# Four places instead of five for the first token tile's expert rows, and the freed memory for six weight tiles loaded early

## The chip, the cores and the metric

The kernel runs on one core of one Trainium2 chip. The metric is the device time of one execution in microseconds (us). The kernel before took 2138.37 us, the median of three runs (2136.37 to 2140.15).

## What is computed

One layer of a decoder block for 256 tokens of width 2048, all in fp32, with weights read from HBM. A token mixer (sparse attention and latent attention, merged by gates) is followed by a channel mixer that looks up experts:

```python
h = rms_norm(x, attn_pre_g[l]) * (1 + sc_a) + sh_a
y = token_mixer(h, positions, w_in[l], ...)          # ends: merged @ w_out
x = x + g_a * rms_norm(y, attn_post_g[l])
h = rms_norm(x, ffn_pre_g[l]) * (1 + sc_f) + sh_f
y = peer_ffn(h, peer_w_q[l], peer_sub_keys[l], peer_u[l], peer_v[l])
x = x + g_f * rms_norm(y, ffn_post_g[l])
```

In `peer_ffn` each token has 8 heads, and each head picks 16 of 16384 experts (two top-16 searches over 128 sub-keys, then a top-16 of their 256 sums). An expert has a row of `u` and a row of `v`, 2048 numbers each:

```python
act = jax.nn.gelu(jnp.einsum('cd,ced->ce', hs, u[es]))
return jnp.einsum('ce,ced->cd', gs * act, v[es])
```

So each of 256 tokens reads 128 rows of `u` and 128 rows of `v`, 8 KB each.

## The kernel before

The tokens are two tiles of 128, one token per partition. "U row i" and "V row i" (U0, V0 and so on below) are the 128 rows that the 128 tokens of a tile pick as their i-th expert (i from 0 to 127): one indirect DMA of 128 x 8 KB = 1.05 MB, issued by GpSimd (`fetch`, line 645) and landed in one place of a ring of places in SBUF.

- A U row is used by VectorE: `dot0` (line 2285) multiplies it with `h2` of its token and sums, which gives one logit, and frees the place (`u0_free`). After each fourth row ScalarE takes the gelu, VectorE multiplies by the gates (`coefs`, line 2280), and ScalarE makes four diagonal matrices of the results (line 1013).
- A V row is used by TensorE: `v_row0` (line 1665) multiplies each diagonal matrix with the V row, in four pieces of 512 columns (8 recorded matmuls), adds into PSUM, and frees the place (`v0_free`).

The order of the work is written out by hand; each engine runs its own list, and semaphores tie them.

*First tile's projections.* TensorE takes 96 weight tiles of 128 x 1024 fp32 (0.524 MB each) for the first token tile, numbered 0 to 95: 0 to 31 the branch projections, 32 to 63 `w_out`, 64 to 95 the queries (`peer_w_q`). SyncE loads them into a ring of eight places, `wide`, at `o_w`; a tile is loaded when the tile eight before it has been used (`w_used`). Tile i lies in place (i + 2) mod 8, so 94 and 95 lie in the places 0 and 1, at the head of `o_w`. `mix(0, i)` is TensorE's step for tile i. Between tiles 63 and 64 the first tile's `h2` is made (`h2_ready`).

*Slots.* After that TensorE and VectorE walk through 132 slots (`SLOTS`). In slot s VectorE does `dot0(s)` (the first slots are shifted a little by `DOTS_AT`: slot 6 does rows 6 to 9), and TensorE does V row s - 4; V rows 0 to 2 go ahead of the slots, among the last queries (`EARLY_V`). The rest of a slot is work of the second token tile: its attention in slots 5 to 60, then its own 96 weight tiles, two in a slot. For these SyncE has a ring of four places, `wide2`, at `o_p`, which it starts to fill when the second tile's attention is done.

*GpSimd's order.* For i from 5 to 127 GpSimd fetches `V_BEFORE[i]` V rows (one, but none for i = 10 to 12 and two for i = 14 to 16) and then U row i. Each fetch waits for its place. The five U places and five V places are parts of SBUF that fall free at different times; the first fetches therefore wait for different semaphores. All fetches stand in one queue: one that waits holds up those behind it.

*Second tile's rows.* When all 128 U rows are fetched, the second tile's rows follow, 128 of U and 128 of V, in rings of eight places: three new ones and the first tile's five as they fall free. No other matmuls of weight lie beside them.

## Time and profile before

| | |
|---|---|
| Median of three runs | 2138.37 us (2136.37 to 2140.15) |
| Profiled execution, its own time | 2141.02 us |
| Its span, as profiled | 2139.0 us |
| TensorE busy | 1915.0 us (90%), 5111 matmuls |
| VectorE busy | 1177.4 us (55%) |
| GpSimd busy | 778.3 us (36%) |
| ScalarE busy | 389.0 us (18%) |
| HBM read and written | 818.37 MB and 2.13 MB, 384 GB/s over the span |

How to read it: busy time is the time in which an engine has an instruction in work; TensorE's is modelled, since matmuls overlap. The page's second section cuts the span in 40 slices of 53.5 us. "SPq" in a timeline is SyncE's queue issuing a DMA. A bracket behind a row is the idle time of the engine before it and what ended it. The DMA rate, in GB/s, is what all 16 DMA engines of the core moved.

### The profile page before, as it was taken

How to read it: one execution, taken by the hardware profiler on the slowest of the kernel's cores; microseconds unless marked ns; L12 is line 12 of the kernel's file. 1: busy time of each engine (PE TensorE's matmuls, PEld its weight loads, DVE VectorE, ACT ScalarE, POOL GpSimd, SP SyncE). 2: the span in 40 equal slices, each digit the busy share in tenths (PEclk: the TensorE clock that was granted, in tenths of full speed). 3: DMA queues.
4: the chain of work that ended last, by engine and by line, in shares of the span. 5: the costliest groups of instructions: out<-in, count | busy, mean ns of one | idle time of the engine just before them, and what ended most of it. 6: DMA issues, size and time to landing. Idle time of an engine off the chain costs nothing.

```text
span 2139.0 us, 15927 instructions
## 1 busy us (share of the span) xinstructions
PE 1915.0 (90%) x5111; PEld 881.8 (41%) x5111; DVE 1177.4 (55%) x2076; ACT 389.0 (18%) x994; POOL 778.3 (36%) x711
## 2 busy tenths in 40 slices
PE   5999999999999899999999999997778778778687
PEld 3444454444445345555444334443333333233233
DVE  5778557724112567768344446345655655655645
ACT  3111021122211134344010112111201101101101
POOL 4322131100000345666222343337364464464453
PEclk9999999999999999999999999999889889889889
DMA  9999969966796999999999999999999999999998
GB/s 343 367 377 398 372 243 379 370 243 224 284 343 233 380 388 410 418 421 421 416 417 418 417 417 420 417 419 422 421 421 421 422 416 422 422 422 422 422 422 353
DMA packets 161760, 821.41 MB, mean 384 GB/s; under 512 B 17152, under 2 KB 23648, under 8 KB 87068
## 3 DMA queue, kind: packets, MB, share of 16 engines
q0 software_dynamic: 92304, 637.58, 72.8%
q1 hardware_dynamic: 67492, 182.12, 23.4%
q10 hardware_dynamic: 1896, 0.86, 0.1%
q8 instruction: 36, 0.59, 0.1%
q14 instruction: 32, 0.26, 0.0%
HBM read 818.37 MB, written 2.13 MB: 384 GB/s over the span
## 4 chain that ended last, share of the span: by engine, by line
PE 53%; DMA 34%; POOL 6%; issue 5%; DVE 2%; ACT 0%; SPq 0%; POOLq 0%; DVEq 0%; ACTq 0%
PE PS L1170 15%; PE PS L1665 13%; DMA arena<-in_peer_v_dram,idx_now 10%; PE PS L1626 10%; DMA arena<-in_peer_u_dram,idx_now 9%; POOL arena L645 5%; PE PS L1728 5%; DMA arena<-in_ada_w_dram 5%; DMA arena<-in_peer_w_q_dram 3%; DMA arena<-in_w_out_dram 2%; DMA arena<-in_w_branch_mla_dram 2%; PE PS L1376 1%; PE PS L1594 1%; DVE arena L1799 1%; DMA arena<-in_w_branch_nsa_dram 1%
## 5 line engine op out<-in xcount | busy, mean ns | idle before, releaser
L1728 PE MATMUL PS<-arena 128*128 128x512 f32 x1008 | 486.6, 646 | 137.5 <-DMA arena<-in_peer_v_dram,idx_now 135.8
L645 POOL DMA_INDIRECT arena<-in_peer_v_dram,idx_now x255 | 352.0, 1380 | 596.3 <-PE PS L1665 336.9
L1665 PE MATMUL PS<-arena 128*128 128x512 f32 x1024 | 471.2, 604 | 21.2 <-DMA arena<-in_peer_v_dram,idx_now 21.1
L2312 DVE CUSTOM_DVE_ANT_0 arena<-arena 128x2048 f32<-128x2048 f32 x128 | 291.7, 2291 | 251.2 <-DMA arena<-in_peer_u_dram,idx_now 251.1
L2285 DVE CUSTOM_DVE_ANT_0 arena<-arena 128x2048 f32<-128x2048 f32 x128 | 292.6, 2290 | 187.6 <-DMA arena<-in_peer_u_dram,idx_now 185.3
L1728 PEld LDWEIGHTS PS<-arena 128*128 128x128 f32 x1008 | 207.1, 208 | 417.0 <-issue 386.4
L645 POOL DMA_INDIRECT arena<-in_peer_u_dram,idx_now x256 | 308.8, 1206 | 145.6 <-issue 70.7
L1626 PE MATMUL PS<-arena 128*128 128x512 f32 x688 | 319.6, 607 | 18.2 <-DMA arena<-in_peer_w_q_dram 8.6
L1170 PE MATMUL PS<-arena 128*128 128x512 f32 x720 | 319.2, 593 | 1.4 <-ACT arena L773 1.4
L1665 PEld LDWEIGHTS PS<-arena 128*128 128x128 f32 x1024 | 191.7, 193 | 253.8 <-issue 220.8
L1626 PEld LDWEIGHTS PS<-arena 128*128 128x128 f32 x688 | 127.7, 192 | 192.7 <-issue 144.5
L1170 PEld LDWEIGHTS PS<-arena 128*128 128x128 f32 x720 | 133.3, 190 | 149.3 <-issue 144.9
L1844 DVE SCALAR_TENSOR_TENSOR arena<-arena,csil 128x2048 f32<-128x2048 f32 x60 | 141.0, 2349 | 18.9 <-DMA arena<-in_ada_w_dram 17.7
L558 POOL DMA_DIRECT2D arena<-in_ada_w_dram x64 | 33.9, 530 | 289.8 <-DVE arena L1844 209.0
L1232 PE MATMUL PS<-arena 128*128 128x512 f32 (+1 forms) x320 | 133.0, 573 | 4.9 <-DVE arena L1779 4.8
L1799 DVE SCALAR_TENSOR_TENSOR arena<-arena,csil 128x512 f32<-128x512 f32 x120 | 90.2, 752 | 20.5 <-DMA arena<-in_ada_w_dram 16.2
L1140 ACT ACTIVATE act_g<-dots 128x4 f32<-128x4 f32 x32 | 6.6, 205 | 498.0 <-DVE dots L2312 498.0
L1013 ACT ACTIVATE arena<-ident,coef 128x128 f32<-128x128 f32 x256 | 81.7, 389 | 81.9 <-DVE coef L2280 81.9
L1232 PEld LDWEIGHTS PS<-arena 128*128 128x128 f32 x320 | 60.6, 193 | 71.3 <-issue 65.6
L546 POOL DMA_DIRECT2D arena<-in_ada_w_dram x64 | 48.0, 754 | 87.8 <-DVE arena L1799 80.7
L640 POOL COPY idx_now<-idx_next 128x16 uint32<-128x16 uint32 x16 | 5.4, 337 | 195.6 <-DVE idx_next L2193 195.6
L2008 DVE CUSTOM_DVE_ANT_0 arena<-PS,causal 128x128 f32<-128x128 f32 (+1 forms) x96 | 30.4, 354 | 67.4 <-PE PS L1376 41.5
(296 smaller groups left out, 1184.5 us busy)
## 6 DMA issues: line engine op xcount, KB each, us to landing
arena<-in_ada_w_dram POOLq DMA_DIRECT2D x64, 1024.0 KB, 8.0
arena<-in_w_in_dram SPq DMA_DIRECT2D x112, 512.0 KB, 8.3
arena<-in_ada_w_dram POOLq DMA_DIRECT2D x64, 512.0 KB, 12.6
arena<-in_w_out_dram SPq DMA_DIRECT2D x64, 512.0 KB, 9.1
arena<-in_peer_w_q_dram SPq DMA_DIRECT2D x64, 512.0 KB, 10.3
arena<-in_w_branch_nsa_dram SPq DMA_DIRECT2D x32, 512.0 KB, 10.0
arena<-in_w_branch_mla_dram SPq DMA_DIRECT2D x32, 512.0 KB, 10.2
arena<-in_x_dram SPq DMA_DIRECT2D x4, 1024.0 KB, 7.9
```

The source lines that it names most:

```text
L546: pool.dma_start(place[:, :, seg, :], ada_v[:, j:j + rows_, c0:c0 + s * P]).then_inc(ada_in[n % ADA_SLOTS], 16)
L645: pool.indirect_dma_start(dst, None, tab, bass.IndirectOffsetOnAxis(ap=idx_now[:, now, e:e + 1], axis=0)).then_inc(landed, 16)
L1013: nc.scalar.activation(diag[e % 8], ident[:, :], ACT.Copy, scale=coef[:, e:e + 1]).then_inc(diag_ready, 1)
L1170: ins = nc.tensor.matmul(PS[:, bank + t, 0:cols], lhs[:, kk, t * P:(t + 1) * P], wring[:, m % WSLOTS, k, 0:cols], start=(kk == 0), stop=(k ...
L1232: ins = nc.tensor.matmul(PS[:, bank + t, 0:cols], hT[:, kk, t * P:(t + 1) * P], wring[:, m % WSLOTS, i, 0:cols], start=(kk == k1), stop=(k ...
L1626: ins = nc.tensor.matmul(PS[:, 4 + a % 2 * 2 + b, :], lhs[:, k, :], tile[:, b * NC:(b + 1) * NC], start=first, stop=last)
L1665: ins = nc.tensor.matmul(PS[:, k, :], diag[i % 8], Vrow0[i % RING0][:, k * NC:(k + 1) * NC], start=(i == 0), stop=False, skip_group_check= ...
L1728: ins = nc.tensor.matmul(PS[:, 4 + k, :], diag[e % 8], Vrow[e % RING][:, k * NC:(k + 1) * NC], start=(first and e == 0), stop=False, skip_ ...
L1799: ins = v.scalar_tensor_tensor(out=part, in0=w, scalar=csil[:, j:j + 1], in1=part, op0=ALU.mult, op1=ALU.add)
L1844: ins = v.scalar_tensor_tensor(out=acc, in0=w, scalar=csil[:, j:j + 1], in1=acc, op0=ALU.mult, op1=ALU.add)
L2285: v.tensor_tensor_reduce(row, row, h2[0], 1.0, 0.0, ALU.mult, ALU.add, dots[:, i % TOPK:i % TOPK + 1]).then_inc(u0_free, 1)
L2312: v.tensor_tensor_reduce(row, row, h2[1], 1.0, 0.0, ALU.mult, ALU.add, dots[:, e:e + 1]).then_inc(u_free, 1)
```

## The change

The first tile's rings have four places, not five (`RING0`). Two places go from the first tile's rows, those at `o_f` and `o_e`; a U place takes the head of the weight ring `o_w`, where a V place was. The freed 2 x 8 KB of each partition hold the second tile's weight tiles 0 to 3 (`w_ahead`). Query tiles 94 and 95 of the first tile (`w_last`) are loaded to a part of SBUF at `o_f + 8 * KW` that was used for `ys` before, so that the head of `o_w` falls free earlier. SyncE loads two of the four ahead of tile 56 and the other two, with `w_last`, ahead of tile 74. The second tile's own loads then begin with tile 4, and its ring of eight rows begins with four new places. Since V rows are issued as `i - RING0`, V row i - 4 now stands before U row i, where V row i - 5 stood.

GpSimd's list of the first fetches, before (u_dram and v_dram are the tables of U and V rows; the first row here is U4):

```order
L645 DMA arena<-in_peer_u_dram,idx_now 128x2048 [waits x1_ready_t0]
L645 DMA arena<-in_peer_v_dram,idx_now 128x2048 [waits w_used]
L645 DMA arena<-in_peer_u_dram,idx_now 128x2048 [waits u0_free]
L645 DMA arena<-in_peer_v_dram,idx_now 128x2048 [waits w_used]
L645 DMA arena<-in_peer_u_dram,idx_now 128x2048 [waits u0_free]
L645 DMA arena<-in_peer_v_dram,idx_now 128x2048 [waits w_used]
L645 DMA arena<-in_peer_u_dram,idx_now 128x2048 [waits u0_free]
L645 DMA arena<-in_peer_v_dram,idx_now 128x2048 [waits w_used]
L645 DMA arena<-in_peer_u_dram,idx_now 128x2048 [waits u0_free]
L645 DMA arena<-in_peer_v_dram,idx_now 128x2048 [waits w_used]
L645 DMA arena<-in_peer_u_dram,idx_now 128x2048 [waits u0_free] x4
L645 DMA arena<-in_peer_v_dram,idx_now 128x2048 [waits v0_free]
```

and with the change (the first row here is U3, the second V0):

```order
L660 DMA arena<-in_peer_u_dram,idx_now 128x2048 [waits w_used]
L660 DMA arena<-in_peer_v_dram,idx_now 128x2048 [waits w_used]
L660 DMA arena<-in_peer_u_dram,idx_now 128x2048 [waits u0_free]
L660 DMA arena<-in_peer_v_dram,idx_now 128x2048 [waits w_used]
L660 DMA arena<-in_peer_u_dram,idx_now 128x2048 [waits u0_free]
L660 DMA arena<-in_peer_v_dram,idx_now 128x2048 [waits w_used]
L660 DMA arena<-in_peer_u_dram,idx_now 128x2048 [waits u0_free]
L660 DMA arena<-in_peer_v_dram,idx_now 128x2048 [waits w_used]
L660 DMA arena<-in_peer_u_dram,idx_now 128x2048 [waits u0_free]
L660 DMA arena<-in_peer_v_dram,idx_now 128x2048 [waits v0_free]
L660 DMA arena<-in_peer_u_dram,idx_now 128x2048 [waits u0_free]
L660 DMA arena<-in_peer_v_dram,idx_now 128x2048 [waits v0_free]
```

V4 and V5, which wait for TensorE to have used V0 and V1 (`v0_free`), now stand ahead of U8 and U9; before, V4 waited for the weight ring alone and V5 stood ahead of U13.

SyncE's list around the first tile's `w_out` and query tiles, before:

```order
L498 DMA arena<-in_w_out_dram 128x1024 [waits w_used] x24
L495 DMA arena<-in_peer_w_q_dram 128x2x512 [waits w_used] x16
L498 DMA arena<-in_peer_w_q_dram 128x1024 [waits w_used] x16
L517 DMA arena<-mod_rows 16x512 [waits weighed]
L521 DMA arena<-in_w_branch_nsa_dram 128x1024 x4
```

and with the change:

```order
L513 DMA arena<-in_w_out_dram 128x1024 [waits w_used] x16
L506 DMA arena<-in_w_branch_nsa_dram 128x1024 [waits w_used]
L506 DMA arena<-in_w_branch_nsa_dram 128x1024
L513 DMA arena<-in_w_out_dram 128x1024 [waits w_used] x8
L510 DMA arena<-in_peer_w_q_dram 128x2x512 [waits w_used] x10
L500 DMA arena<-in_peer_w_q_dram 128x1024 [waits h2_ready_t0]
L500 DMA arena<-in_peer_w_q_dram 128x1024
L502 DMA arena<-in_w_branch_nsa_dram 128x1024 x2
L510 DMA arena<-in_peer_w_q_dram 128x2x512 [waits w_used] x6
L513 DMA arena<-in_peer_w_q_dram 128x1024 [waits w_used] x14
L532 DMA arena<-mod_rows 16x512 [waits weighed]
L536 DMA arena<-in_w_branch_nsa_dram 128x1024 x4
```

Two loads of the second tile's weights (`w_branch_nsa`) stand within the `w_out` loads; the two last query tiles and two more of the second tile's stand behind the tenth narrow query load, after a wait for the first tile's `h2`.

The diff, without semaphore names and the places where a tile is looked up by its consumers alone:

```diff
@@ -41,7 +41,8 @@
 
 PH, NK, TOPK = 8, 128, 16
 RING = 8
-RING0 = 5
+RING0 = 4
+AHEAD = 4
 BATCH = 4
 
 WSLOTS = 8
...
@@ -187,6 +188,8 @@
 
         wide = at(o_w, WSLOTS, 2 * NC)
         wide2 = at(o_p, W2SLOTS, 2 * NC)
+        w_last = at(o_f + 8 * KW, 2, 2 * NC)
+        w_ahead = [at(o, 2 * NC) for o in (o_f, o_f + 4 * KW, o_e, o_e + 4 * KW)]
         merged = [at(o_a, D), at(o_e + 24 * KW, D)]
         mergedT = [at(o_a + 8 * KW, KD, P), at(o_f + 16 * KW, KD, P)]
         y, h2T = merged, mergedT
...
@@ -213,15 +216,15 @@
         onehot = at(o_t, 2, TOPK, TOPK)
         diag = [at(o_e + 16 * KW + P * i, P) for i in range(8)]
         sq_junk = at(o_s, NC)
-        early_u = [o_f, o_c, o_e, o_e + 8 * KW, o_a]
-        early_v = [o_w + 8 * KW, o_w + 16 * KW, o_w + 24 * KW, o_w, o_a + 8 * KW]
+        early_u = [o_c, o_e + 8 * KW, o_a, o_w]
+        early_v = [o_w + 8 * KW, o_w + 16 * KW, o_w + 24 * KW, o_a + 8 * KW]
         Urow0 = [at(o, D) for o in early_u]
         Vrow0 = [at(o, D) for o in early_v]
         first_free = (PH * TOPK) % RING0
-        slots_u = [o_p, o_p + 8 * KW, o_p + 16 * KW] + early_u[first_free:] + early_u[:first_free]
-        slots_v = [o_f + 16 * KW, o_f + 24 * KW, o_i] + early_v[first_free:] + early_v[:first_free]
+        slots_u = [o_p, o_p + 8 * KW, o_p + 16 * KW, o_f] + early_u[first_free:] + early_u[:first_free]
+        slots_v = [o_f + 16 * KW, o_f + 24 * KW, o_i, o_e] + early_v[first_free:] + early_v[:first_free]
         Urow = [at(o, D) for o in slots_u]
-        slot_sem = [5, 6, 7] + [(first_free + i) % RING0 for i in range(RING0)]
+        slot_sem = [4, 5, 6, 7] + [(first_free + i) % RING0 for i in range(RING0)]
         sem_base = [16 * len(range(i, PH * TOPK, RING0)) if i < RING0 else 0 for i in slot_sem]
         Vrow = [at(o, D) for o in slots_v]
 
...
@@ -366,7 +371,7 @@
 
         def w2_landed(i):
 
-            return 16 * (len(range(i % W2SLOTS, W_BR + MIX, WSLOTS)) + i // W2SLOTS + 1)
+            return 16 * (len(range(i % W2SLOTS, W_BR + MIX - 2, WSLOTS)) + (i - AHEAD) // W2SLOTS + 1)
 
         def gate_tile(c_):
             return W_G0 + 8 * c_ if c_ < 6 else W_G5 + 8 * (c_ - 6)
...
@@ -375,7 +380,7 @@
         TURN_AT = (20, 22, 36, 38)
         Q_AT = ((73, 82, MIX, MIX + 2), (82, 88, MIX, MIX + 2))
         SC_AT = ((74, 85, MIX + 1, MIX + 3), (85, 91, MIX + 1, MIX + 3))
-        QUERIES, NARROW = 64, 16
+        QUERIES, NARROW, LAST_AT, AHEAD_AT = 64, 16, 74, 56
         GATE_F_AT = (40, 44)
         LAST_OUT = 4
         SHARED, HALF = TOPK - BATCH, D // 2
...
@@ -487,8 +492,18 @@
                 sp.dma_start(dst, mod_dram[k, :].partition_broadcast(P)).then_inc(landed, 16)
 
 
-            for i in range(MIX):
+            for i in range(MIX - 2):
                 m = W_BR + i
+                if i == LAST_AT:
+                    sp.wait_ge(h2_ready[0], 1)
+                    for k in range(2):
+                        sp.dma_start(w_last[:, k, :], mix_src(MIX - 2 + k)).then_inc(w_last_in, 16)
+                    for k in range(AHEAD // 2, AHEAD):
+                        sp.dma_start(w_ahead[k], mix_src(k)).then_inc(w_ahead_in, 16)
+                if i == AHEAD_AT:
+                    sp.wait_ge(w_used, W_BR + 32)
+                    for k in range(AHEAD // 2):
+                        sp.dma_start(w_ahead[k], mix_src(k)).then_inc(w_ahead_in, 16)
                 sp.wait_ge(w_used, m - WSLOTS + 1)
                 if QUERIES <= i < QUERIES + NARROW:
                     n, k = (i - QUERIES) // 8, 2 * ((i - QUERIES) % 8)
...
@@ -510,18 +525,18 @@
                     sp.dma_start(shift_k[0:4, :, :], mod_dram[1, :].rearrange("(a b d) -> b a d", a=4, b=4)).then_inc(shift_in, 16)
                 if i == 39:
                     sp.wait_ge(merged_ready, 4)
-                    sp.dma_start(X[0], x_v[:, 0, :]).then_inc(x2_in[0], 16)
+                    sp.dma_start(X[0], x_v[:, 0, :]).then_inc(x2_in, 16)
 
 
             sp.wait_ge(weighed, 2 * UNITS)
-            sp.dma_start(mod_rows[0:16, :], mod_dram[0:4, :].rearrange("k (n c) -> (k n) c", n=4)).then_inc(row_in[1], 16)
-            for i in range(MIX):
-                if i >= W2SLOTS:
+            sp.dma_start(mod_rows[0:16, :], mod_dram[0:4, :].rearrange("k (n c) -> (k n) c", n=4)).then_inc(row_in, 16)
+            for i in range(AHEAD, MIX):
+                if i >= AHEAD + W2SLOTS:
                     sp.wait_ge(w2_used, i - W2SLOTS + 1)
                 sp.dma_start(wide2[:, i % W2SLOTS, :], mix_src(i)).then_inc(w_landed[i % W2SLOTS], 16)
                 if i == 39:
                     sp.wait_ge(merged_ready, 8)
-                    sp.dma_start(X[1], x_v[:, 1, :]).then_inc(x2_in[1], 16)
+                    sp.dma_start(X[1], x_v[:, 1, :]).then_inc(x2_in, 16)
             sp.wait_ge(out_ready, 1)
             sp.wait_ge(v_free, (PH - 1) * TOPK + SHARED + 3)
             sp.dma_start(out_v[:, 0, :], X[0]).then_inc(out_stored, 16)
...
@@ -653,20 +668,20 @@
                 if i >= RING0:
                     pool.wait_ge(u0_free, i - RING0 + 1)
                 elif i == 0:
-                    pool.wait_ge(merged_ready, 4)
+                    pool.wait_ge(y_mul, 4)
                 elif i == 1:
-                    pool.wait_ge(y_mul, 4)
-                elif i == 4:
+                    pool.wait_ge(h2_ready[0], 1)
+                elif i == 2:
                     pool.wait_ge(x1_ready[0], 1)
                 else:
-                    pool.wait_ge(h2_ready[0], 1)
+                    pool.wait_ge(w_used, W_BR + MIX - 8)
                 fetch(u_tab, Urow0[i % RING0], u % 2, e, u_in[i % RING0])
 
             def v_row0(i):
                 if i >= RING0:
                     pool.wait_ge(v0_free, i - RING0 + 1)
                 else:
-                    pool.wait_ge(w_used, W_BR + MIX - 6 + 2 * min(i, 3))
+                    pool.wait_ge(w_used, W_BR + MIX - 6 + 2 * i)
                 fetch(v_tab, Vrow0[i % RING0], i // TOPK % 2, i % TOPK, v_in[i % RING0])
 
             n_v = 0
...
@@ -683,7 +698,7 @@
                     pool.wait_ge(free, r * TOPK + ((b + 1) * BATCH - RING))
                 pool.sem_inc(pool_passed, 1)
                 for e in range(b * BATCH, (b + 1) * BATCH):
-                    if first and 3 <= e < RING:
+                    if first and RING - RING0 <= e < RING:
                         pool.wait_ge(u0_free if tab is u_tab else v0_free, PH * TOPK - RING + e + 1)
                     if halved and e == TOPK - 1:
                         pool.wait_ge(idx_ready, 2 * PH + 1)
...
@@ -1568,9 +1583,15 @@
                 ins.then_inc(row_made, 1)
 
             def tile_of(t, i):
+                if t == 0 and i >= MIX - 2:
+                    pe.wait_ge(w_last_in, 32)
+                    return w_last[:, i - (MIX - 2), :]
                 if t == 0:
                     tile_ready(W_BR + i)
                     return wide[:, (W_BR + i) % WSLOTS, :]
+                if i < AHEAD:
+                    pe.wait_ge(w_ahead_in, 16 * AHEAD)
+                    return w_ahead[i]
                 pe.wait_ge(w_landed[i % W2SLOTS], w2_landed(i))
                 return wide2[:, i % W2SLOTS, :]
 
```

## Rows read from the trace of the kernel before

**Rows 1.** The page: DMA rate in 40 slices; row fetch queue: packets, MB, share.
```profile
GB/s 343 367 377 398 372 243 379 370 243 224 284 343 233 380 388 410 418 421 421 416 417 418 417 417 420 417 419 422 421 421 421 422 416 422 422 422 422 422 422 353
...
q0 software_dynamic: 92304, 637.58, 72.8%
```

**Rows 2.** Stretches: busy us by engine, clock, share and rate of DMA.
```profile
665.00:680.00 15.00, 15.00 (x66) 10.65 (x66) 8.51 (x11) 4.30 (x8) 0.00 (x0) 0.85 0.25 79
680.00:705.00 25.00, 25.00 (x69) 11.70 (x68) 8.61 (x34) 2.75 (x5) 0.24 (x2) 1.00 0.85 284
780.00:795.00 15.00, 15.00 (x55) 7.58 (x54) 6.87 (x21) 7.30 (x17) 7.66 (x8) 1.00 0.85 303
795.00:820.00 25.00, 25.00 (x85) 12.53 (x84) 17.26 (x44) 7.84 (x20) 13.52 (x9) 1.00 0.98 397
820.00:930.00 110.00, 110.00 (x377) 55.50 (x375) 83.16 (x199) 43.38 (x107) 66.86 (x46) 1.00 1.01 420
1430.00:2115.00 685.00, 534.64 (x1134) 228.27 (x1133) 393.18 (x604) 83.19 (x228) 356.33 (x283) 0.89 1.01 421
```

**Rows 3.** SyncE's queue, in time: start, length, line, operation; landing of line 498, 705:740.
```profile
634.80 5.48 SPq L498 DMA_DIRECT2D arena<-in_w_out_dram  x4
...
674.67 12.38 SPq L495 DMA_DIRECT2D arena<-in_peer_w_q_dram  x8
...
DMA to landing us min/median/max: 8.6/15.8/21.1
```

**Rows 4.** VectorE in time: the normalised first tile gets its shift.
```profile
672.96 2.35 DVE L2145 SCALAR_TENSOR_TENSOR arena<-arena,cstat 128x2048 f32<-128x2048 f32 x1 [1.81 <-PE PS L1638]
```

**Rows 5.** GpSimd in time: row fetches, with idle time and releaser in brackets.
```profile
704.96 1.01 POOL L645 DMA_INDIRECT arena<-in_peer_u_dram,idx_now  x1 [0.91 <-POOL idx_now L640]
...
721.05 0.95 POOL L645 DMA_INDIRECT arena<-in_peer_v_dram,idx_now  x1 [10.05 <-PE PS L1626]
...
734.47 0.95 POOL L645 DMA_INDIRECT arena<-in_peer_v_dram,idx_now  x1 [6.61 <-PE PS L1626]
...
769.81 0.94 POOL L645 DMA_INDIRECT arena<-in_peer_v_dram,idx_now  x1 [7.32 <-PE PS L1665]
...
807.41 2.79 POOL L645 DMA_INDIRECT arena<-in_peer_u_dram,idx_now  x1 [0.30 <-issue]
```

**Rows 6.** Line 645: all V fetches, landing of all; landing in 850:900.
```profile
L645 POOL DMA_INDIRECT arena<-in_peer_v_dram,idx_now x255: 942/951/3057, 721.1 to 2112.0; - x128
...
DMA to landing us min/median/max: 7.3/21.7/35.6
...
DMA to landing us min/median/max: 7.5/11.1/12.9
```

**Rows 7.** VectorE: dots of U4, U9, U23, a wait, coefficients of U20 to U23.
```profile
730.88 2.29 DVE L2285 CUSTOM_DVE_ANT_0 arena<-arena 128x2048 f32<-128x2048 f32 x1 [1.03 <-DMA arena<-in_peer_u_dram,idx_now]
...
758.12 2.29 DVE L2285 CUSTOM_DVE_ANT_0 arena<-arena 128x2048 f32<-128x2048 f32 x1 [2.66 <-DMA arena<-in_peer_u_dram,idx_now]
...
837.50 2.28 DVE L2285 CUSTOM_DVE_ANT_0 arena<-arena 128x2048 f32<-128x2048 f32 x1
...
842.10 0.17 DVE L2019 RECIPROCAL srec<-ssum 128x2 f32<-128x2 f32 x1 [2.31 <-ACT arena L858]
...
846.81 0.16 DVE L2280 TENSOR_TENSOR coef<-act_g,gate_now 128x4 f32<-128x4 f32 x1 [0.25 <-issue]
```

**Rows 8.** TensorE in time: last query tiles, then V0, V3, V7 and V19.
```profile
730.41 5.85 PE L1626 MATMUL PS<-arena 128*128 128x512 f32 x8 [0.89 <-DMA arena<-in_peer_w_q_dram]
...
741.10 3.60 PE L1665 MATMUL PS<-arena 128*128 128x512 f32 x8
...
763.16 6.37 PE L1665 MATMUL PS<-arena 128*128 128x512 f32 x8
...
785.85 3.70 PE L1665 MATMUL PS<-arena 128*128 128x512 f32 x8
...
845.90 3.70 PE L1665 MATMUL PS<-arena 128*128 128x512 f32 x8
```

More of the change, by code:

```diff
@@ L290, in build @@
         w_landed = [sem(f"w_landed{i}") for i in range(WSLOTS)]
+        w_last_in, w_ahead_in = sem("w_last_in"), sem("w_ahead_in")
         w_used = sem("w_used")
@@ L319, in each_tile @@
             return [sem(f"{name}_t{t}") for t in range(NT)]
-        row_in, x2_in = each_tile("row_in"), each_tile("x2_in")
+        row_in, x2_in = sem("row_in"), sem("x2_in")
         scale_in, shift_in, row_made, row_out = sem("scale_in"), sem("shift_in"), sem("row_made"), sem("row_out")
@@ L325, in build @@
         h2_ready, x1_ready = each_tile("h2_ready"), each_tile("x1_ready")
-        y_part, v_rest = sem("y_part"), sem("v_rest")
+        y_part = sem("y_part")
+        v_rest = sem("v_rest")
         y_gsq, diag_made, h2b_ready = sem("y_gsq"), sem("diag_made"), sem("h2b_ready")
@@ L501, in _ @@
                     sp.wait_ge(mod_stored, 16)
-                    mod_row(gate_a_row[0], 0, row_in[0])
+                    mod_row(gate_a_row[0], 0, row_in)
                 if i == 15:
@@ L1558, in gate_row @@
                 if half == 0:
-                    pe.wait_ge(row_in[1], 16)
+                    pe.wait_ge(row_in, 32)
                 else:
@@ L2084, in y_gated @@
                 else:
-                    dve.wait_ge(row_in[0], 16)
+                    dve.wait_ge(row_in, 16)
                 dve.wait_ge(y_sq, 4 * t + n + 1)
@@ L2102, in _ @@
             y_gated(0, 1)
-            dve.wait_ge(x2_in[0], 16)
+            dve.wait_ge(x2_in, 16)
             dve.wait_ge(scale_in, 16)
@@ L2260, in second_projections @@
                     dve.wait_ge(y_mul, 8)
-                    dve.wait_ge(x2_in[1], 16)
+                    dve.wait_ge(x2_in, 32)
                     v.scalar_tensor_tensor(out=X[1], in0=y[1], scalar=rstd[:, RMS_Y:RMS_Y + 1], in1=X[1], op0=ALU.mult,
```

## The prediction

> **What bounds the kernel now.** I read the page's line of DMA rates first. From slice 16 on it stands at 416 to 422 GB/s in every slice, to the tail [rows 1]; before, it is lower in several slices. The stretches say the same: 79 GB/s from 665 to 680 us and 284 from 680 to 705, then 420 from 820 to 930 and 421 from 1430 to 2115 [rows 2]. I take 421 as the rate of a full queue: a row of 1.049 MB takes 2.49 us of it, a weight tile of 0.524 MB 1.25 us. What stands behind the first row fetch at 704.96 [rows 5] is therefore a fixed list of bytes; the end comes when they have landed, and only holes in the DMA add to it. Three stretches hold the holes that matter: 665 to 705 (weights alone, TensorE bound), 780 to 795 (303 GB/s, a loss of 15 x (1 - 303/421) = 4.2 us) and 795 to 820 (397, a loss of 1.4 us) [rows 2].
>
> Why there are holes at 780 to 820 is to be seen in TensorE's and GpSimd's rows. TensorE is busy for all of 820 to 930 (110.00 of 110.00) [rows 2], and V7 begins at 785.85, V19 at 845.90, so a slot takes 60.05/12 = 5.00 us [rows 8]. A slot fetches one U and one V row, 4.98 us of DMA. So the second tile's attention runs at TensorE's pace, with DMA level to it, and GpSimd's fetches are released by TensorE: V7 is issued at 769.81 after 7.32 us of idleness that TensorE ended [rows 5]. With rings that are full, DMA can't run ahead.
>
> **The loads moved forward.** Six tiles (3.15 MB, 7.5 us of a full queue) go from the full stretch to 634 and 676.
> - *Two ahead of tile 56.* SyncE issues four loads from 634.80, one per 1.7 us [rows 3]; that is TensorE's pace of 1.72 us a tile, 305 GB/s. Two more loads delay tile 56 by 2 x 1.25 = 2.5 us and the delay is worked off. A tile lands some 5 us after issue in a ring that turns in 8 x 1.72 = 13.8 us, so it has about 7 us to spare. Cost 0; if that cover were gone, up to 2.5 us.
> - *Four ahead of tile 74.* They wait for `h2_ready`, which comes at 672.96 + 2.35 = 675.31 [rows 4]. The narrow loads 72 to 79 go out in 12.38 us from 674.67 [rows 3], so tile 74 goes at about 678.1: the wait is already over, though behind it stand the rest of the queries. Its four loads take 5.0 us of DMA, where 7 us are spare, and the top-16 that releases the first fetch depends on tiles up to 73 only. Cost 0; bounds 0 to 5 us (all four late on TensorE).
>
> **The first fetches.** With the change U3 waits for tile 87 to be used, about 717 (an estimate: V0 goes when tile 89 is used, 721.05, and two tiles take 3.4 us), and V0 goes as before. U0 to U2 (3.1 MB) and tiles 88 to 93 share the queue till then, so it stays full. In this stretch weight tiles took up to 21.1 us to land [rows 3]; 94 and 95 were the worst, and are now there. TensorE's last waits go: tiles 93 and 94 took 5.85 us from 730.41, V0 came at 741.10 [rows 8]; now it comes at 730.41 + 5.85 + 1.7 + 1.2 = 739.2.
>
> What counts is when U9 lands, because slot 6 makes the dots of U6 to U9 and TensorE's V3, the first of the attention, waits behind it. Now: U9 is used at 758.12 when it lands, V3 begins at 763.16 [rows 7, 8]. Ahead of it landed 10 U rows, V0 to V4 and tiles 88 to 95: 15 x 1.049 + 8 x 0.524 = 19.9 MB. With the change V5 stands ahead of U9 too, and 94 and 95 don't: 16 x 1.049 + 6 x 0.524 = 19.9 MB. The two cancel. There is one hole: V2 still waits for tile 93 (734.47 [rows 5]). U4 landed at 730.88 [rows 7]; now V0 is there in its place, then U4, V1, U5 until 738.4, and V2 lands at 734.47 + 7.3 (the least landing time [rows 6]) = 741.8 instead of 740.9. So U9 comes 0.9 to 1.2 us later, and with it all that goes at TensorE's pace. I take **+1.2 us**; bounds -3 to +3, because V3 took 6.37 us where V7 took 3.70 [rows 8]: the clock was at its half level after TensorE's idleness, and idleness is shifted here.
>
> **The lead.** In the stretch at TensorE's pace the number of rows issued is set by what TensorE has used. Before, V row j goes when V row j - 5 is used and U row j + 5 behind it; now V row j when V row j - 4 is used, and U row j + 4 behind it. For U that is a lead of 8 rows on TensorE instead of 10, for V 4 instead of 5. Rows in flight are one fewer (a row lands 8 to 9 us after issue instead of 11.1 [rows 6]), so the rows landed at a given point of TensorE's list are two fewer: 2 x 2.49 = **+5.0 us** of DMA work that is still to be done. The price shows as wider holes at 770 to 805: V7 can't go before V3 is used (769.8), U14 stands behind V7 and V8 (775, an estimate: V4 is used at 773.4, V8 goes, then U14), and by my count of 2.49 us a row from U9 on, U13 has landed by 771. The same point has four weight tiles more: 4 x 1.25 = **-5.0 us**. The 2.5 us of 94 and 95 are gone by then, since V5 filled them. Sum of both: 0.
>
> **Less slack.** Before, a row lands 11.1 us after issue where 7.5 is the least [rows 6]: 3.6 us of queue cover a late issue. Now about 1.2 us. GpSimd's issues take 0.95 us but up to 3.06 [rows 6]; the one at 807.41 took 2.79 [rows 5]. Each that is over 1.2 us late opens a hole. A hole makes later rows land later against TensorE, which gives back slack, so it stops when the slack is near 3 us again: at most about 2.4 us. Bounds: 0, and +8 if TensorE is held as well. I take **+1.4 us**.
> The Trainium skill (SBUF — State Buffer, "Who interferes with whom") says that a VectorE instruction with two SBUF inputs holds up a GpSimd instruction that reads SBUF, until it ends. By that rule, the long issue at 807.41 is one under a dot, the trace agrees with its 2.79 us, and the ring of four meets the same dots with less slack. Another page (DMA: Bandwidth & Descriptors, "Anatomy of one DMA") fits 2.0 us + bytes/436e3, 4.4 us for a row; the trace has never under 7.3 us, and the measurement decides. By 4.4 us the hole at V2 and the loss of slack would both be gone and the sum would be near 0.
>
> **Everything later.** The U ring isn't the limit in the second tile's mix (7.5 us a slot, where TensorE needs 6.9), and V row 4b waits for the dot of U row 4b + 3, which lands one row ahead of it instead of three: TensorE runs some 4 us behind landing, in a ring that turns in 30 us. Covered. From 1430 the eight places are as before.
>
> **Sum:** +1.2 + 5.0 - 5.0 + 1.4 = +2.6 us on the profiled execution: 2141.02 + 2.6 = 2143.6, which is 2.65 over the median of the runs shown; on that median, 2138.37 + 2.6 = **2141.0 us**. A measurement of this kernel tells 0.2% (4.3 us) from no change.
>
> **Rivals.**
> 1. *The moved bytes count in full.* If the end is bytes at a full rate alone, all six tiles are saved: 2138.4 - 7.5 = 2130.9. For it: 421 GB/s to the end. Against: the holes at 780 to 820, with VectorE and DMA ready and TensorE at 100%. Chance 0.11.
> 2. *TensorE is held in the attention (slower).* U row 4b + 3 must be dotted, and coefficients and diagonals made, before V row 4b. Dot 23 began at 837.50 and the coefficients came at 846.81; between the dot's end (839.8) and them lie 7.0 us, of which 2.31 were a wait for ScalarE, 4.7 work [rows 7]. V20 followed V19 at about 849.9. Now U23 goes behind V19, when V15 is used: V19's start less four slots, 825.9, + 3.7 + 0.3 + 1.25 = 831.1 [rows 8], and lands 9.1 us later, 840.2, or 842 with the slack lost. The dot ends at 844.5, the coefficients come at 849.2: just in time. If it is 1 us late in each of the seven fours of 790 to 930, TensorE, DMA and end slip by 7 us: 2138.4 + 1.2 + 7 = 2146.6. It decides from U rows landing 2 us later than I think. Chance 0.23.
> 3. *TensorE starts the attention earlier*, because the half clock after idleness falls before V3: -2.7 us there, 2138.4 - 2.7 + 1.4 = 2137.1. Chance 0.07.
> 4. *The early loads don't fit*: the four ahead of tile 74 come in too late for TensorE, the queries slip by up to 5 us and the gain of `w_ahead` is lost: 2145. Chance 0.05.
>
> **Chances.** The forecast has 0.54, with 2137 to 2145 as its own range. Faster by over 0.2% (under 2134.1): rival 1, 0.11. Slower (over 2142.7): most of rivals 2 and 4 (0.20 + 0.03) and 0.10 of the forecast's upper side, 0.33. The rest, 0.56, is no change that can be told. Eight in ten: 2134 to 2149.
>
> **What would show it.** The first fetch at 705 and V0 at 721; `h2_ready` before SyncE's wait; last query tiles without waits; U9's dot at 759 to 760; the DMA rate of 765 to 805 clearly under the 780 to 795 loss of before, 10 us and more in sum; TensorE without waits, V19 at about 847; no wait for weights at the mix's first tiles; from 1430 everything shifted by 2 to 3 us. The prediction is wrong if U9 lands before 756, if TensorE shows waits for diagonals in 800 to 930, or if the second half of the kernel has new holes.

## The result, and the profile after

The changed kernel takes 2144.23 us (median of ten runs, 2140.60 to 2151.33); the kernel before, over its ten runs, 2138.76 (2136.37 to 2141.59). The ratio is 1.0026, with a 95% interval of 1.0018 to 1.0034. The time lies in the range that was given and 3.2 us above the forecast of 2141.0. The ratio lies just beyond the 0.2% from which a change can be told, with an interval that reaches from under it to over it: a little slower, which had a chance of 0.33 against 0.56 for "the same". The medians differ by 5.5 us, twice the 2.6 that were forecast.

The profiled execution of after took 2142.60 us (span 2140.9), that of before 2141.02 (2139.0). The pair differs by 1.6 us and the medians by 5.5, because the profiled run of after is one of its faster ones and that of before one of its slower. The stretches of after, in the columns of [rows 2]:

```profile
634.00:665.00 31.00, 31.00 (x73) 13.28 (x72) 9.79 (x21) 5.75 (x17) 0.00 (x0) 1.00 0.89 321
...
665.00:680.00 15.00, 14.56 (x69) 9.35 (x70) 9.21 (x13) 4.51 (x9) 0.00 (x0) 1.00 0.47 156
680.00:705.00 25.00, 25.00 (x72) 11.98 (x71) 8.62 (x34) 3.33 (x6) 1.70 (x3) 1.00 1.00 374
765.00:820.00 55.00, 55.00 (x189) 27.51 (x189) 36.62 (x95) 21.46 (x52) 28.08 (x21) 1.00 0.89 327
820.00:930.00 110.00, 109.26 (x373) 54.83 (x374) 81.37 (x196) 41.99 (x105) 52.15 (x46) 1.00 1.01 422
1275.00:1335.00 60.00, 60.00 (x136) 25.85 (x135) 37.06 (x60) 12.15 (x25) 30.60 (x21) 0.89 0.99 392
1430.00:2115.00 685.00, 536.71 (x1135) 230.01 (x1134) 394.53 (x604) 83.38 (x228) 360.96 (x287) 0.88 1.01 421
```

Of before, three that [rows 2] doesn't have:

```profile
634.00:665.00 31.00, 31.00 (x70) 13.04 (x68) 10.45 (x23) 5.36 (x16) 0.00 (x0) 0.96 0.85 295
...
765.00:820.00 55.00, 55.00 (x181) 27.25 (x180) 37.38 (x98) 19.67 (x49) 25.49 (x19) 0.97 0.95 377
...
1275.00:1335.00 60.00, 56.92 (x135) 24.64 (x134) 38.78 (x59) 14.67 (x30) 26.01 (x20) 0.94 1.01 420
```

The last number, the rate, gives the loss of a stretch as its length x (1 - rate/421). In us:

| stretch | before | after |
|---|---|---|
| 634 to 665 | 9.3 | 7.4 |
| 665 to 705 | 20.3 | 12.2 |
| 765 to 820 | 5.7 | 12.3 |
| 1275 to 1335 | 0.1 | 4.1 |
| the other six stretches from 705 to 1445 | 5.7 | 6.9 |
| sum | 41.1 | 42.9 |

The sum rises by 1.8 us, as the spans do (1.9). So the holes account for the pair of profiles in full: 10 us are won before the first fetch and lost again in two later stretches, one foreseen (765 to 820) and one not (1275 to 1335). From 1445 on nothing differs (15 us before that have 398 GB/s, where before has 422; that loss of 0.9 us is in the other six stretches). In both losing stretches TensorE is busy throughout (55.00 of 55.00, 60.00 of 60.00) while the DMA rate falls, as it would with fetches that are paced by a full ring. What the fetches wait for is to be read from GpSimd's rows.

GpSimd's list in the first of them (columns: start, length, engine, line, operation; line 660 is the fetch):

```profile
703.20 1.01 POOL L660 DMA_INDIRECT arena<-in_peer_u_dram,idx_now  x1 [0.91 <-POOL idx_now L655]
...
718.72 0.95 POOL L660 DMA_INDIRECT arena<-in_peer_v_dram,idx_now  x1 [2.49 <-PE PS L1647]
...
727.67 0.95 POOL L660 DMA_INDIRECT arena<-in_peer_v_dram,idx_now  x1 [2.73 <-PE PS L1647]
...
764.83 1.68 POOL L660 DMA_INDIRECT arena<-in_peer_v_dram,idx_now  x1 [6.71 <-PE PS L1686]
768.70 0.94 POOL L660 DMA_INDIRECT arena<-in_peer_v_dram,idx_now  x1 [2.19 <-PE PS L1686]
769.95 2.82 POOL L660 DMA_INDIRECT arena<-in_peer_u_dram,idx_now  x1 [0.30 <-issue]
```

V7 waits until V3 is used, V8 until V4 is, and U14 goes behind both at 769.95. In before, V7 went at 758.24 and U14 behind it, without a wait for TensorE:

```profile
761.54 0.95 POOL L645 DMA_INDIRECT arena<-in_peer_u_dram,idx_now  x1 [0.30 <-issue]
```

So U14 is fetched 8.4 us later than before. The fetch at 769.81 in [rows 5], which the prediction calls V7, is V8: it is the one that V3 releases there (V3 ends at 769.53).

In the second stretch, before and then after:

```profile
1300.37 2.75 POOL L645 DMA_INDIRECT arena<-in_peer_v_dram,idx_now  x1 [1.24 <-PE PS L1665]
1303.42 0.95 POOL L645 DMA_INDIRECT arena<-in_peer_u_dram,idx_now  x1 [0.30 <-issue]
1309.33 0.95 POOL L645 DMA_INDIRECT arena<-in_peer_v_dram,idx_now  x1 [4.95 <-PE PS L1665]
...
1316.63 0.94 POOL L645 DMA_INDIRECT arena<-in_peer_u_dram,idx_now  x1 [0.31 <-issue]
```

```profile
1299.02 0.95 POOL L660 DMA_INDIRECT arena<-in_peer_v_dram,idx_now  x1 [1.23 <-PE PS L1686]
1300.28 2.72 POOL L660 DMA_INDIRECT arena<-in_peer_u_dram,idx_now  x1 [0.30 <-issue]
1309.63 0.95 POOL L660 DMA_INDIRECT arena<-in_peer_v_dram,idx_now  x1 [6.63 <-PE PS L1686]
...
1316.93 0.95 POOL L660 DMA_INDIRECT arena<-in_peer_u_dram,idx_now  x1 [0.31 <-issue]
```

TensorE at the same place of after, then its clock in 1290 to 1310 (last but two) and the 10 us behind:

```profile
1298.68 4.52 PE L1569 MATMUL PS<-arena,ident 16*128 16x512 f32 x8
1303.13 6.23 PE L1686 MATMUL PS<-arena 128*128 128x512 f32 x8
...
1310.94 3.60 PE L1686 MATMUL PS<-arena 128*128 128x512 f32 x8
```

```profile
1290.00:1310.00 20.00, 20.00 (x39) 8.08 (x39) 13.53 (x20) 0.37 (x2) 8.17 (x7) 0.71 1.01 424
...
1310.00:1320.00 10.00, 10.00 (x33) 4.98 (x31) 5.94 (x12) 4.65 (x10) 4.28 (x4) 1.00 0.90 316
```

TensorE has 4.52 us of other work and then a V row that takes 6.23 us, partly at the half clock; the fetch that it releases goes at 1309.63. GpSimd has stood still since 1303.00 (1300.28 + 2.72). Two V fetches lie 10.6 us apart (1299.02 and 1309.63). In before the gap is 9.0 us (1300.37 to 1309.33), one more V row is in flight, and the DMA stays at 420; in after it falls to 316 behind the gap, a loss of 2.5 us. Another 1.3 us are lost ahead of the gap, in 1275 to 1290 (384 GB/s); their cause is not traced.

### The profile page after: what moved, and what is told of

The parts are those of the page before. It is cut to its first block, busy times and chain, and to the rows that moved or that the text cites. A ratio compares the mean times of both kernels' runs of the same rounds, so it can differ in the third digit from the quotient of the medians.

```text
span 2140.9 us, 15915 instructions
## 1 busy us (share of the span) xinstructions
PE 1914.3 (89%) x5111; PEld 881.7 (41%) x5111; DVE 1178.7 (55%) x2076; ACT 388.9 (18%) x994; POOL 762.3 (36%) x711
## 4 chain that ended last, share of the span: by engine, by line
PE 52%; DMA 33%; POOL 6%; issue 4%; DVE 4%; ACT 0%; DVEq 0%; POOLq 0%; SPq 0%; ACTq 0%
PE PS L1185 14%; PE PS L1686 13%; DMA arena<-in_peer_u_dram,idx_now 11%; PE PS L1647 10%; DMA arena<-in_peer_v_dram,idx_now 7%; POOL arena L660 6%; PE PS L1749 5%; DMA arena<-in_w_out_dram 3%; DMA arena<-in_peer_w_q_dram 3%; DMA arena<-in_ada_w_dram 3%; DMA arena<-in_w_branch_mla_dram 2%; PE PS L1247 2%; PE PS L1615 1%; DVE arena L1820 1%; PE PS L1391 1%
## 5 line engine op out<-in xcount | busy, mean ns | idle before, releaser
L660 POOL DMA_INDIRECT arena<-in_peer_v_dram,idx_now x255 | 335.1, 1314 | 605.9 <-PE PS L1686 378.6
## 6 DMA issues: line engine op xcount, KB each, us to landing
arena<-in_peer_w_q_dram SPq DMA_DIRECT2D x64, 512.0 KB, 10.2
```

Source lines behind the costliest of these rows:

```text
L660: pool.indirect_dma_start(dst, None, tab, bass.IndirectOffsetOnAxis(ap=idx_now[:, now, e:e + 1], axis=0)).then_inc(landed, 16)
```

## The experiments

Each was timed against the kernel before, with ratios to it; the kernel before had medians of 2138.7 to 2139.6 us beside them, so a time here is best compared by its ratio. The diffs show the lines that matter, and "..." stands for lines left out. "Hole 1" is the loss in 765 to 820, "hole 2" that in 1275 to 1335, both worked out as above.

**The loads alone, undone.** The four tiles of the second tile are loaded as before; the small rings and the moved query tiles stay.

```diff
-AHEAD = 4
+AHEAD = 0
...
```

> The changed kernel with rings of four and the two last query tiles early, but the second tile's weight tiles 0 to 3 loaded when its attention is done, as before. Theory 'lead' (two rows fewer landed when TensorE paces the fetches, made up for by four tiles that are already there): the four tiles are worth 4 x 1.25 = 5.0 us, so this is 5 us over the changed kernel, some 10 us over the one before (2149), with the same DMA holes at 765 to 820 us. Rival 'the early loads are what costs' (they are late or in the way): equal to or faster than the changed kernel, near 2139 to 2144.

2148.80 us, ratio 1.0047 (1.0033 to 1.0061). The four tiles are worth 2148.8 - 2144.2 = 4.6 us, so the gain of the change is near its full 5.0, though the two intervals (1.0033 to 1.0061, and 1.0018 to 1.0034 of after) just meet and leave its size open by some 3 us. What costs more than that is the rings. Hole 1 is 55 x (1 - 319/421) = 13.3.

**The query tiles alone, in rings of five.**

```diff
...
+                if i == 74:
+                    sp.wait_ge(h2_ready[0], 1)
+                    for k in range(2):
+                        sp.dma_start(w_last[:, k, :], mix_src(MIX - 2 + k)).then_inc(w_last_in, 16)
...
```

> The kernel before with rings of five, and only the two last query tiles loaded early beside the ring. Theory 'lead': the 2.5 us of DMA that it frees at 715 to 738 us are lost again in the holes at 780 to 820, since TensorE's pace sets the fetches there, so 0 to -1 us against before; TensorE's waits for the last tiles go and V0 comes 2 us earlier. Rival 'bytes in the full stretch': -2.5 us (ratio 0.9988).

2136.55 us, ratio 0.9991 (0.9982 to 1.0000). A gain of some 2 us, which lies between what the two theories expect and nearer to the bytes; the interval just touches 1. Hole 1 is 55 x (1 - 399/421) = 2.9, where before has 5.7.

**Four tiles less, in rings of five.** What the bytes are worth when nothing else changes. The kernel leaves these four loads out and computes with stale data in their place.

```diff
-            for i in range(MIX):
-                if i >= W2SLOTS:
+            for i in range(4, MIX):
+                if i >= 4 + W2SLOTS:
...
```

> The kernel before with rings of five, in which the second tile's weight tiles 0 to 3 are not loaded at all (its projections use stale data in their place; this part of the computation is left out). It prices the four tiles alone, without the smaller rings. Theory 'lead': all of their DMA time is saved, -5.0 us (ratio 0.9977). Rival 'they are hidden anyway', as where the start of the second tile's projections waits for TensorE: -1 to 0 us.

2133.28 us, ratio 0.9975 (0.9966 to 0.9984): 5.4 us, within the noise the 5.0 of four tiles at 421 GB/s.

**Rings of four, but V row i - 5 ahead of U row i.** The first test of the order.

```diff
+LAG0 = 5
...
-                for _ in range(V_BEFORE.get(i, 1) if i >= RING0 else 0):
+                for _ in range(V_BEFORE.get(i, 1) if i >= LAG0 else 0):
...
```

> The changed kernel with its rings of four, but V row i - 5 ahead of U row i in GpSimd's list, as before the change, where the change put V row i - 4. A U row then stands behind a V row that TensorE frees one slot earlier. Theory 'lead through GpSimd's order': one of the two lost rows comes back, the holes at 765 to 820 shrink from 12.4 to about 10 us, those at 1275 to 1335 mostly go, -2.5 to -5 us against the changed kernel. Rival 'the number of places is what costs': same time as the changed kernel within 1 us, same holes.

2139.95 us, ratio 1.0006 (0.9997 to 1.0015): 4.3 us less than after. Its stretches:

```profile
765.00:820.00 55.00, 55.00 (x191) 27.86 (x190) 37.76 (x94) 21.64 (x55) 32.14 (x22) 1.00 0.96 361
...
1275.00:1335.00 60.00, 60.00 (x147) 26.61 (x146) 38.57 (x59) 14.47 (x29) 28.90 (x21) 0.97 1.02 420
```

Hole 1 falls from 12.3 to 7.8, with the same places: in this order each U row stands one V fetch further ahead, so it is on its way when that V fetch begins to wait. Hole 2 is gone in this profile, and its V fetches there lie at most 7.3 us apart (1295.33 and 1302.58), but here TensorE's clock in 1290 to 1310 was full:

```profile
1290.00:1310.00 20.00, 20.00 (x59) 9.39 (x58) 13.16 (x23) 4.82 (x10) 8.69 (x8) 1.00 1.01 421
```

So that part of the 4.3 us may be the order's or the clock's. That the V place matters there is better supported: at a clock of 0.74 the kernel with four U and five V places, below, has 420 GB/s in 1275 to 1335, with V fetches at most 8.9 us apart (1300.67 and 1309.52), where after has 392 at 0.71. After differs from it in the order and the loads too; the cleaner pair are the two kernels below with V row i - 5, of which the one with four V places has 410 (at 0.83) and the one with five 420, a difference of 1.5 us in one profile each.

**Which ring?** The kernel before with one place less, for U rows in one and for V rows in the other, with the order V row i - 5 kept and all loads as before.

```diff
-RING0 = 5
+RU, RV, LAG0 = 4, 5, 5
...
-        early_u = [o_f, o_c, o_e, o_e + 8 * KW, o_a]
+        early_u = [o_c, o_e, o_e + 8 * KW, o_a]
...
```

> The kernel before with four places for U rows and five for V rows; GpSimd's order (V row i - 5 ahead of U row i) and all weight loads as before. Theory 'V rows set the lead': a U place is free as soon as VectorE has made its dot, one or two slots ahead of TensorE, so a fourth place is enough nearly everywhere: 0 to +1 us against before. Rival 'each place is worth its row': one row less is landed, +2.5 us (ratio 1.0012).

```diff
-RING0 = 5
+RU, RV, LAG0 = 5, 4, 5
...
-        early_v = [o_w + 8 * KW, o_w + 16 * KW, o_w + 24 * KW, o_w, o_a + 8 * KW]
+        early_v = [o_w + 8 * KW, o_w + 16 * KW, o_w + 24 * KW, o_a + 8 * KW]
...
```

> The kernel before with five places for U rows and four for V rows, the same order (V row i - 5 ahead of U row i), weight loads as before. Theory 'V rows set the lead': V row j waits until TensorE has used V row j - 4, and U row j + 5 stands behind it, so one V row and one U row fewer are out: +2.5 to +5 us (ratio 1.0012 to 1.0023), holes of 9 to 11 us at 765 to 820. Rival 'each place is worth its row': +2.5 us as for the U place.

Four U places: 2139.04 us, ratio 1.0001 (0.9992 to 1.0010). Four V places: 2143.53, ratio 1.0021 (1.0012 to 1.0030). 765 to 820, four U places and then four V places:

```profile
765.00:820.00 55.00, 55.00 (x186) 27.44 (x185) 37.74 (x95) 21.78 (x55) 28.56 (x22) 1.00 0.99 395
```

```profile
765.00:820.00 55.00, 55.00 (x181) 27.21 (x180) 37.83 (x100) 19.68 (x49) 25.97 (x19) 0.97 0.93 345
```

The rate falls to 345 (hole 1: 9.9 us) only where the V place is gone. And the first fetches of that kernel show why:

```profile
769.93 0.95 POOL L647 DMA_INDIRECT arena<-in_peer_v_dram,idx_now  x1 [11.24 <-PE PS L1668]
...
780.37 0.96 POOL L647 DMA_INDIRECT arena<-in_peer_v_dram,idx_now  x1 [5.08 <-PE PS L1668]
781.63 0.95 POOL L647 DMA_INDIRECT arena<-in_peer_u_dram,idx_now  x1 [0.30 <-issue]
```

The row at 769.93 is V7: GpSimd stands 11.24 us for TensorE, with U rows behind it. A V place is freed by TensorE, the late engine; a U place by VectorE, when it has made the dot. The V place is worth 4.5 us, the U place nothing that can be told. That doesn't make the fifth U place idle. Of GpSimd's U fetches in 820 to 1275, with four U places (columns: busy, mean ns | idle before and what ended it):

```profile
L647 POOL DMA_INDIRECT arena<-in_peer_u_dram,idx_now x75 | 82.4, 1099 | 211.8 <-DVE dots L2286 202.0 <-issue 8.2 <-POOL idx_now L642 1.6
```

They wait 202.0 us for dots, where in before 5.0 us go to dots and 217.4 of the V fetches' wait to TensorE. With four U places VectorE has become the one that releases, only not later than TensorE did.

**One step further, in rings of four.** After, with `LAG0 = 6`.

> The changed kernel (rings of four, six tiles early) with V row i - 6 ahead of U row i. Theory 'the order sets the lead until a place is missing': U row i now waits for the dot of U row i - 4, which comes at about the same time as TensorE frees the V row before it, so at most 1 us more is won than with V row i - 5: ratio 1.000 to 1.0006. Rival 'one more step back is worth as much as the first': -4 us more, ratio 0.9987.

2136.61 us, ratio 0.9984 (0.9975 to 0.9993). Its stretches:

```profile
765.00:820.00 55.00, 55.00 (x191) 27.92 (x190) 37.33 (x101) 19.79 (x50) 30.47 (x23) 1.00 0.99 399
...
1275.00:1335.00 60.00, 57.44 (x130) 24.87 (x129) 34.96 (x56) 13.68 (x29) 31.55 (x21) 0.89 0.96 389
```

Hole 1 falls further, to 55 x (1 - 399/421) = 2.9, and there is a hole in 1275 to 1335 again (4.6 us), but not the same one. GpSimd waits here for VectorE, with U rows:

```profile
1306.01 0.94 POOL L661 DMA_INDIRECT arena<-in_peer_u_dram,idx_now  x1 [8.07 <-DVE dots L2307]
...
1313.85 0.94 POOL L661 DMA_INDIRECT arena<-in_peer_u_dram,idx_now  x1 [5.50 <-DVE dots L2307]
```

With V row i - 6 it is the U rows that are held up in this stretch. Rings of five with the same order lose 0.9 us there; but four U and five V places (below) lose 0.7, at a clock of 0.91 in 1290 to 1310 where this profile has 0.77, so the clock may have its part again. The time is 3.3 us less than with 5 and 7.6 less than after. I had expected at most 1 us more; the other theory, another step of the same size, was nearer. So the version with small rings beats the kernel before once the order is changed as well.

**Rings of five, the query tiles moved, and V row i - 6.**

```diff
-RING0 = 5
+RU, RV, LAG0 = 5, 5, 6
...
```

> Rings of five, the two last query tiles early, and V row i - 6 ahead of U row i. Theory 'the order sets the lead': one U row more is out while TensorE paces the fetches, the holes at 765 to 820 shrink from 2.9 to about 1 us; -3 to -4 us against before, 1 to 2 us better than rings of five with the last tiles early alone. Rival 'the places are the limit': the same as that kernel, ratio 0.999.

2134.30 us, ratio 0.9976 (0.9965 to 0.9986), the fastest version that does all the work. Against the same rings and loads without the new order (2136.55) the order gives 2.3 us by the medians, though the two intervals overlap (up to 0.9986, and from 0.9982). In its profile hole 1 is closed:

```profile
765.00:820.00 55.00, 55.00 (x189) 27.56 (x188) 38.30 (x97) 22.67 (x56) 32.10 (x23) 1.00 1.01 421
...
1275.00:1335.00 60.00, 57.51 (x128) 24.75 (x129) 37.03 (x57) 14.48 (x29) 30.10 (x20) 0.89 1.01 415
```

**Do the early loads disturb anything?** After, with the four tiles never loaded and stale data in their place.

```diff
...
-                    for k in range(AHEAD // 2, AHEAD):
-                        sp.dma_start(w_ahead[k], mix_src(k)).then_inc(w_ahead_in, 16)
...
```

> The changed kernel in which the second tile's weight tiles 0 to 3 are never loaded (its projections take stale data for them; this part of the computation is left out). Theory 'the early loads are free': same time as the changed kernel, ratio to before 1.0026, at most 1 us under it. Rival 'they are in the way' (they delay SyncE's query loads or TensorE): 2 to 5 us faster than the changed kernel, 1.0005 to 1.0015.

2142.98 us, ratio 1.0017 (1.0008 to 1.0026), 1.25 us under after by the medians and 2 us by the ratios, with intervals that overlap (1.0018 to 1.0034 of after). The early loads cost between 0 and some 4 us, so this run doesn't choose between the two expectations.

**The idle place put to use.** Four U places and five V places, the query tiles moved, two tiles ahead in the U place's memory, V row i - 6; then the same with i - 7.

```diff
-RING0 = 5
+RU, RV, LAG0 = 4, 5, 6
...
+        w_ahead = [at(o, 2 * NC) for o in (o_f, o_f + 4 * KW)]
...
```

> A version drawn from the runs: four U places, five V places, V row i - 6 ahead of U row i, the two last query tiles early, and in the one freed U place the second tile's weight tiles 0 and 1 (loaded ahead of tile 56). Theory 'a U place is idle memory, a V place is not': the sum of the parts, -4.7 us (rings of five, last tiles early, V row i - 6) and -2.5 us for two tiles: ratio 0.9965 to 0.997. Rival 'with V row i - 6 the fourth U place is the limit': no better than rings of five, 0.9976 or more.

> The same with V row i - 7 ahead of U row i. A U row then waits for the dot of U row i - 4 where TensorE has used V row i - 12: VectorE, not TensorE, releases it nearly always. Theory: the order has nothing left to give and V rows go out late, 0 to +3 us against V row i - 6. Rival 'the further back the better': -1 to -2 us more.

With 6: 2135.35 us, ratio 0.9982 (0.9973 to 0.9992), no better than the five places (2134.30), though two tiles are loaded early, 2.5 us by their bytes; so with V row i - 6 the fifth U place seems to be worth about what the tiles give, but no run has it alone. With 7: 2146.98, ratio 1.0030 (1.0018 to 1.0042). TensorE in 820 to 1275, V rows, with 7 (columns as above), and then with 6:

```profile
L1683 PE MATMUL PS<-arena 128*128 128x512 f32 x589 | 269.9, 601 | 18.0 <-DMA arena<-in_peer_v_dram,idx_now 17.6
```

```profile
L1683 PE MATMUL PS<-arena 128*128 128x512 f32 x599 | 273.1, 599 | 7.0 <-DMA arena<-in_peer_v_dram,idx_now 6.7
```

With 7 TensorE waits longer for V rows, and GpSimd for dots:

```profile
1222.35 2.75 POOL L658 DMA_INDIRECT arena<-in_peer_u_dram,idx_now  x1 [11.44 <-DVE dots L2303]
```

Here the U fetch stands at the head for 11.44 us and the V rows behind it are late: the same fault with the rings changed over. In 1275 to 1335 this profile loses 5.1 us (385 GB/s), again with GpSimd waiting for dots (8.82 and 7.93 us), five V places or not. In these runs a U place was free of cost only as long as the order didn't ask U rows to run further ahead.

## Why the prediction was right, and where not

The total was right within 3.2 us, and in part by luck. The two largest terms were near what the runs give; three others were wrong: the first fetches in sign, less slack, which wasn't paid, and "everything later", which was put at nothing. Their errors (-3.0, -1.4 and +4.0 us) nearly cancel.

**The early loads, right for the most part.** SyncE passes both new waits at once, two of the loads at 634 and two at 676:

```profile
634.27 0.91 SPq L506 DMA_DIRECT2D arena<-in_w_branch_nsa_dram  x2
...
675.03 0.94 SPq L500 DMA_DIRECT2D arena<-in_peer_w_q_dram  x2
676.01 1.51 SPq L502 DMA_DIRECT2D arena<-in_w_branch_nsa_dram  x2
677.57 2.56 SPq L510 DMA_DIRECT2D arena<-in_peer_w_q_dram  x3
```

The rate of 665 to 680 rises from 79 to 156 and of 680 to 705 from 284 to 374. Cost 0 was predicted, 0 to some 4 us is what the runs allow. "Last query tiles without waits" was nearly so: one wait of 1.67 us is left where they begin (725.41).

**The first fetches, wrong in sign.** U9's dot was to come 1.2 us later. The dot, and V0 and V3, in the columns of [rows 7] and [rows 8]:

```profile
754.60 2.29 DVE L2306 CUSTOM_DVE_ANT_0 arena<-arena 128x2048 f32<-128x2048 f32 x1 [2.66 <-DMA arena<-in_peer_u_dram,idx_now]
```

```profile
725.41 5.42 PE L1647 MATMUL PS<-arena 128*128 128x512 f32 x12 [1.67 <-DMA arena<-in_peer_w_q_dram]
...
732.00 3.60 PE L1686 MATMUL PS<-arena 128*128 128x512 f32 x8
...
757.64 2.07 PE L1391 MATMUL PS<-arena 64*128 64x256 f32 x4 [9.52 <-DVE smax L2029]
759.64 4.91 PE L1686 MATMUL PS<-arena 128*128 128x512 f32 x8
```

The dot is 754.60 - 703.20 = 51.4 us behind the first fetch, where it was 758.12 - 704.96 = 53.2: 1.8 us earlier. I had taken TensorE's end of the queries, and with it V2's fetch, as unchanged in time. But TensorE waits less for query tiles, and V0 stands on it 28.8 us after the first fetch instead of 36.1. Most of that comes with the moved tiles: with them alone, in rings of five, it is 739.60 - 708.45 = 31.2 us. V2 is fetched 24.5 us behind the first fetch instead of 29.5, so the hole for which I had charged 1 us didn't come (419 to 423 GB/s from 730 to 745). The rest of the 1.8 us is no hole closed: from the first fetch to U9's dot the rate is 407 GB/s in both profiles, and 0.7 MB less moves in that time in after; which bytes, stays open. By its own bound ("wrong if U9 lands before 756") this step failed.

Part of the change in absolute time is chance: the first fetch stands at 703.20 here, at 704.96 in before and between 703.4 and 708.5 in experiments whose work up to there is nearly the same. One profile each can't say more, and the 3.9 us by which the medians differ more than the profiled pair can't be placed in a stretch.

**The lead, near in size, wrong in what it was put down to.** Two rows fewer landed were to cost 5.0 us, four tiles to give 5.0, and the query tiles' 2.5 to be swallowed. The four tiles gave 4.6 in rings of four and 5.4 in rings of five. U14 goes behind V7 and V8 as predicted (at 769.95, not 775, since V3 came earlier). The price of the small rings is the difference of two kernels that are otherwise alike, 2148.80 - 2136.55 = 12.3 us; my terms for it were 5.0 + 2.5 + 1.2 + 1.4 = 10.1. But I had put it down to both rings alike. The runs give the V place 4.5, the U place nothing, and the order i - 4 another 4.3, which costs no memory to undo; some 3.5 us of the 12.3 stay without a part of their own, so the parts may not simply add.

**Less slack, wrong in its mechanism.** There was to be a +1.4 by short holes wherever an issue is late. Landing in 850 to 900 after:

```profile
DMA to landing us min/median/max: 9.3/10.5/11.6
```

Before it was 7.5/11.1/12.9 [rows 6]. The median fell by 0.6 us where I had expected some 2, the least time rose, and 820 to 930 has 422 GB/s: late issues opened no holes there.

**"Everything later: covered", wrong.** It held to 1275, apart from 0.9 us in 1005 to 1035, and not in 1275 to 1335. I had compared averages, the DMA's time for a slot of the mix with TensorE's (7.5 and 6.9 us), and asked of the U ring only. From 1271 to 1314 TensorE has no weight tiles, runs through the landed V rows, and then leaves 10.6 us between two releases. The stretch cost 4.0 us more than before, 2.5 of them behind that gap and 1.3 ahead of it. The trace of before had the sign: two V fetches 9.0 us apart, in a stretch that I didn't query. A hole in this stretch is there in the profiles of four of the five kernels with four places in both rings (after, 2148.80, 2142.98 and 2136.61 us), in the last of them behind dots, and is small (1.6 us) with four V places alone.

**Sum.** Predicted 1.2 + 5.0 - 5.0 + 1.4 + 0 = +2.6. By the holes of the profiles: -10.0 up to 705 (of which 7.5 are the six tiles), +6.6 in hole 1, +4.0 in hole 2, +1.2 elsewhere: +1.8. By the medians +5.5. The step that failed worst is "everything later: covered": it stood at 0 and added 4.0, while the first fetches gave 3.0 more than predicted (-1.8 for +1.2) and the 1.4 for slack wasn't paid. 2.6 + 4.0 - 3.0 - 1.4 = 2.2, near the profiles' 1.8.

**The rivals.** The moved bytes in full (2130.9) is out: only the part up to 705 behaved so. TensorE held in the attention shows in the trace and hardly in time. There is one wait for diagonals of 0.74 us at 924.62, in a stretch with the DMA at 422, and a longer one behind the stretch that I had named:

```profile
1005.13 6.73 PE L1686 MATMUL PS<-arena 128*128 128x512 f32 x8 [3.39 <-ACT arena L1028]
```

From 930 to 1005 TensorE is busy for 69.39 of 75 us, where before it was for all 75; the DMA stays at 421 there, and 1005 to 1035 then loses the 0.9 us named above. So two of the three signs by which the prediction would be "wrong" did appear (U9 early, new holes in the second half), and the third did in small, though the number of the forecast held.

## What to carry to other kernels

When one queue issues for two rings, ask for each ring which engine empties it: the place of the late engine was the lead here, and that of the prompt one spare until the order asked its rows to run further ahead. A change in ring depth that also moves the issue order is two changes, to be timed apart. Look for every stretch in which the late engine releases the fetches, and for the longest gap between two releases in each, not the average; a lead can be paid for in each of them. Before giving a place away or buying one, try the order of issue: one to two steps were worth 2.3 to 7.6 us here, and one step too many cost 11.6.

## What the runs showed of the hardware

Rows and weight tiles shared the DMA with as many packets each, not as many bytes. In 712 to 728 of before, with both waiting, the row queue moved 616 packets and 4.45 MB, the weight queue 617 packets and 2.26 MB: each packet of the rows was about twice as large, and the rows took two thirds of the rate.

With the two last query tiles out of this stretch, V0 stood on TensorE earlier against the first fetch by 5.0 us in rings of five and by 7.3 in after, more than the 2.5 us of their bytes. I had counted the bytes alone. The tiles that were left landed no sooner at first: the first three issued behind the first fetch took 8.6, 10.2 and 12.3 us before and 8.5, 10.1 and 12.2 in after, the next two 15.8 and 17.0 against 12.7 and 13.8. In after only three U rows go out at once where five did, and with five U rows and the tiles moved it is 15.0 and 16.1; one profile each doesn't separate the causes.
